# When VectorE makes the V index of a separately gathered expert row: in the row's own step, or in the next one

## The chip, the cores and the metric

One Trainium2 chip, one core. The metric is device time of one execution in microseconds (us). The kernel before takes 1458.97 us (median of three runs, 1458.47 to 1459.36).

## The reference, cut to what matters

The reference is a chain of two transformer blocks on 256 tokens of width 1024. The change touches only the last part, the mixture of single-vector experts at the end of the second block. There every token has 8 heads, each head picks 16 of 16384 experts, and each expert is one row of `expert_u` and one row of `expert_v` (1024 float32 numbers each, 4 KB):

```
best, pos = lax.top_k(cand, K)                      # K = 16
idx = jnp.take_along_axis(cand_idx, pos, axis=-1)
g = jax.nn.softmax(best, axis=-1)
u = expert_u[idx]
v = expert_v[idx]
act = jax.nn.gelu(jnp.einsum('td,thkd->thk', xt, u))
return jnp.einsum('thk,thkd->td', (g * act), v)
```

For one token and one expert this is a dot product with the U row, a gelu, a weight, and the weighted V row added to the sum. Where the gelu comes out as zero, the V row isn't needed.

## The kernel before, in words

Tokens lie on the 128 partitions, in two blocks of 128. The work of this last stage is cut into 256 "rows": row i = 16n + k is the expert of rank k of group n, where a group is one head of one token block (16 groups, `GROUPS`, of 16 ranks, `EXPK`). The program runs as five separate instruction streams that meet only in semaphores. Per row they do this:

- **GpSimd (POOL)** issues the gathers. There are 8 buffers (`SLOTS`), and row i uses buffer i mod 8. Rows in buffers 1, 4 and 7 (`JOINT`) are fetched in one gather of 8 KB per token, U and V together, from a table that was joined beforehand (`row`, L665). Rows in buffers 0, 2, 3, 5 and 6 are separate: one gather for U (L672), and a later one for V (`row_v`, L682), which skips the tokens whose weight is zero. The V gather of row r stands in POOL's stream six rows later (`V_LAG`), just behind the U gather of row r + 6. It waits until VectorE has made the V index of row r (`rows_picked`), and until TensorE has used the V rows that lay in the same buffer before (`row_used`). A U gather waits until VectorE has done the dot of the row eight earlier (`dot_ready`). The last eight rows are all fetched jointly.
- **VectorE (DVE)** waits for the row to land and multiplies and sums it with the token's vector (`row_dot`, L2596, 1.22 us). Between the dots it does one piece of the top-k selection of a coming group (`top_part`, L2477 to L2548), and for a separate row it makes the V index (`pick_row`): it waits for the weight of the row (`w_ready`), marks the tokens with weight zero (L2605) and adds that mark to the expert number, so that such a token lies beyond the table's end (L2610).
- **ScalarE (ACT)** does for each row a gelu of the dot (L1762), its product with the softmax probability (L1767, this releases `w_ready`), and it spreads the weight of a row over a 128 by 128 diagonal matrix (L1754): that of a joint row in the row's own step, that of a separate row seven steps later. Once per group, behind rank 2 (in group 0 behind rank 10), it does the exponentials of the next group's softmax (`exp_best`, L1747). Exponential and gelu are in different function tables, so a table is loaded before it and another one behind it.
- **TensorE (PE)** multiplies the diagonal with the V row and adds to the sum (`weigh_row` L1288, and L1331 in the rolled loop of rows 144 to 247): a joint row in its own place, a separate row r when row r + 8 has its turn. The order is fixed. In groups 0 to 7 it also makes the queries and scores of later groups in between.

VectorE's order in one step k of group n is written out by hand: the dot of row k; then the V index of row k - 1; then the other pieces (`decode`, `top_part`, at rank 6 or 14 also `probabilities`). So the V index of a row was made behind the dot of the next row.

Of the kernel before, what the change touches and what calls it, by code (L numbers as in the profile page):

```python
# [42 lines left out]
EXPK = 16  # L43
# [5 lines left out]
SLOTS = 8  # L49

JOINT = (1, 4, 7)
# [147 lines left out]
def two_blocks(nc, wstream, x_t, mem_t, cols, const, head_gains, c_rows, positions, w_krope, w_uq, w_ukv,  # L199
               w_rg, w_ig, sub_keys, w_ada, expert_u, expert_v, out):  # L200
    with ExitStack() as ctx:
# [294 lines left out]
        def separate(rows):  # L496

            return rows // SLOTS * (SLOTS - len(JOINT)) + sum(k not in JOINT for k in range(rows % SLOTS))

        def joint(i):  # L500
            return i % SLOTS in JOINT or i >= LAST_FROM
# [194 lines left out]
        def _(pe):  # L696
# [203 lines left out]
            def first_block(layer):  # L900
# [19 lines left out]
                for s, (kind, c, _) in enumerate(FUSED[:-KC]):  # L920
                    u = FUSED_AT[layer] + s
                    if kind == "v":
                        pair_half(bank["v", c | 1], u, c % 2, x)
                    else:
                        product = (lambda: chunk_sum(7, SQ, start_units, 3)) if (layer, s) == (0, 0) else None
                        proj(bank[kind, c], u, x, fresh, by="vec", fine_first=kind == "qm", between=product)
                        fresh = (None, None)
                        if layer and s == 0:
                            chunk_sum(7, steps=3)
                    taken[kind, c] = made["act" if kind == "v" else "vec"]  # L930
                    if kind == "qm":
                        pair_taken[layer, 6 + c] = (("vec", taken[kind, c]), ("act", taken["vm", 1]))
                    for p in range(6):
                        if (kind, c) == (("v", p + 1) if p % 2 == 0 else ("k", p)):
                            pair_taken[layer, p] = (("vec", taken["k", p]), ("act", taken["v", p | 1]))
                    if (kind, c) == ("qm", 1):
                        scale_by_token(layer + 1, RS)
                    if layer == 0 and (kind, c) == ("q", 1):
                        pe.wait_ge(fcum_ready, due(fcum_ready))
                    attend(layer, group_at[s], before, earlier)  # L940
                    if layer == 0 and (kind, c) == ("q", 1):
                        for b in range(NB):
                            mm = pe.transpose(PS[:, FQ_BANK, b * P:(b + 1) * P], FT[:, b * P:(b + 1) * P], ident)
                        mm.then_inc(tile_for["vec"], handed(FQ_BANK, "vec"))
                    before, earlier = group_at[s], before
# [421 lines left out]
        def _(act):  # L1367
# [82 lines left out]
            def first_block(layer):  # L1450
# [42 lines left out]
                for s, (kind, c, _) in enumerate(FUSED[:-KC]):  # L1493
                    if earliest is not None:
                        group_heads(layer, earliest)
                    if earlier is not None:
                        group_turned(layer, earlier)
                    if before is not None:
                        group_exps(layer, before)
                    split_hi(FUSED_AT[layer] + s + 2)  # L1500
                    if layer == 0 and s == 5:
                        forget_gate()
                    if (kind, c) == ("qm", 1):
                        take_scale(layer + 1)
                    elif kind == "v" and c % 2:
                        take_values(slice((c // 2) * T, (c // 2 + 1) * T), value_tile("v", c), layer + 1)
                    before, earlier, earliest = group_at[s], before, earlier
# [305 lines left out]
        def _(ve):  # L1813
# [768 lines left out]
            def probabilities(n):  # L2582
                par = n % 2
                ve.wait_ge(gexp_ready, n + 1)
                ve.reciprocal(gexp[:, par, 18:19], gexp[:, par, 16:17]).then_inc(topk_step, one(topk_step))
                if n >= 2:
                    ve.wait_ge(w_ready, EXPK * (n - 1))
                ve.wait_ge(topk_step, own(topk_step))
                ve.tensor_scalar(prob[:, par, :], gexp[:, par, 0:EXPK], gexp[:, par, 18:19], None,
                                 ALU.mult).then_inc(prob_ready, 1)  # L2590

            def row_dot(i):
                n, k = i // EXPK, i % EXPK
                row = place(i)[:, 0:D]
                ve.wait_ge(row_landed[i % SLOTS], 16 * (i // SLOTS + 1))
                ve.tensor_tensor_reduce(row, row, H2N[n // 8], 1.0, 0.0, ALU.mult, ALU.add,  # L2596
                                        dot[:, n % 2, k:k + 1]).then_inc(dot_ready, 1)

            def pick_row(i):

                n, k, s = i // EXPK, i % EXPK, i % SLOTS
                if joint(i):
                    return
                ve.wait_ge(w_ready, i + 1)
                ve.tensor_scalar(no_row[:, s:s + 1], wts[:, s:s + 1], 0.0, NO_ROW, ALU.is_equal,  # L2605
                                 ALU.mult).then_inc(tokens_marked, 1)
                if i >= SLOTS:
                    ve.wait_ge(v_landed[s], 16 * (i // SLOTS))
                ve.wait_ge(tokens_marked, separate(i + 1))
                ve.tensor_tensor(idx_v[:, s:s + 1], no_row[:, s:s + 1], idx[:, n % 3, k:k + 1],  # L2610
                                 ALU.add).then_inc(rows_picked, 1)

            def gated_sum(b, half=slice(0, 2)):
                cols = slice(half.start * 512, half.stop * 512)
                tmp = soft[:, 0:4 * T][:, cols]
                ve.tensor_tensor(tmp, PS[:, 2 * b + half.start:2 * b + half.stop, :].rearrange("p a e -> p (a e)"), G2[:, cols],
                                 ALU.mult).then_inc(vec_step, one(vec_step))
                ve.wait_ge(vec_step, own(vec_step))
                ve.tensor_tensor(XNAT[:, b, cols], XNAT[:, b, cols], tmp, ALU.add).then_inc(result_ready, 1)
# [6 lines left out]
            for n in range(GROUPS):  # L2626
                if n == 0:
                    probabilities(0)
                if n % 8 == 0:
                    ve.wait_ge(h2_ready, 2 * (n // 8 + 1))  # L2630
                for k in range(EXPK):
                    row_dot(n * EXPK + k)
                    if n or k:
                        pick_row(n * EXPK + k - 1)
                    if n == 0 and k == 0:
                        for q in range(6):
                            decode(0, q, slice(8, EXPK))
                    if n == 0 and 3 <= k < 9:
                        if k == 3:
                            ve.wait_ge(took["act"], QUERIES_FROM + 3)  # L2640
                        for q in range(3 * (k - 3), min(3 * (k - 2), EXPK)):
                            top_part(1, q)
                    if k >= TOPS_FROM and n + 2 < GROUPS:
                        if n < 6 and k == TOPS_FROM:
                            ve.wait_ge(took["act"], SCORES_FROM + 3 * (n + 3))
                        top_part(n + 2, k - TOPS_FROM)
                    elif 0 < n < GROUPS - 1 and k < TOPS_FROM:
                        top_part(n + 1, k + EXPK - TOPS_FROM)
                    if n == 1 and k < KC:
                        ve.tensor_scalar(DGATE[:, k * P:(k + 1) * P], ident, mod[:, 40 + k:41 + k], None,  # L2650
                                         ALU.mult).then_inc(g2diag, one(g2diag))
                    if k == (6 if n else 14) and n + 1 < GROUPS:
                        probabilities(n + 1)
                    if n == 9 and k == 8:
                        ve.wait_ge(took["act"], FINAL_TAKEN)
                        ve.wait_ge(row_used, weighed_by[last_weighed[0]])
                        gated_sum(0)
# [122 lines left out]
```

## Time and profile before

| | |
|---|---|
| median of three runs | 1458.97 us |
| profiled execution, its own time | 1459.09 us |
| its span | 1457.5 us |
| PE busy | 1373.4 us (94%) |
| DVE busy | 1150.3 us (79%) |
| ACT busy | 785.1 us (54%) |
| POOL busy | 499.1 us (34%) |
| DMA | 542.73 MB, mean 372 GB/s |

The profile is of one execution. The row stage runs from about 859 us (first gather) to 1449 us (last dot), 40% of the span. POOL is idle before the stage but for plain copies; within it, it issues 411 gathers. DMA is the mean busy share of the 16 DMA engines, and GB/s what they moved. A wait in the trace is written as [us idle <-what ended it] behind the instruction that it held up; for a wait on several semaphores the one named is the last to come by the profile.

### The profile page before, as it was taken

The numbers are of one execution on the slowest core, as the hardware profiler recorded it, in microseconds if no ns is written. First come the engines' busy times: TensorE is split into PE (matmuls) and PEld (weight loads), VectorE is DVE, ScalarE is ACT, GpSimd is POOL, SyncE is SP. The second block draws the span as 40 slices with busy tenths as digits, with TensorE's granted clock in tenths as the row PEclk, the third lists the DMA queues.
The fourth block names the chain that finished last, engine by engine and source line by source line (L and its number), as shares of the span: only waits on it lengthen the run. The fifth ranks groups of instructions, "written<-read, shape, count | busy, mean of one in ns | idle before, by whom it ended". The sixth has DMA issues, their size and how long they took to land.

```text
span 1457.5 us, 25909 instructions
## 1 busy us (share of the span) xinstructions
PE 1373.4 (94%) x8512; PEld 1067.3 (73%) x8512; DVE 1150.3 (79%) x2772; ACT 785.1 (54%) x1768; POOL 499.1 (34%) x600
## 2 busy tenths in 40 slices
PE   9999999999999999999999999999898998888878
PEld 9898999999989999998998985444454433333333
DVE  7777788878878888678799779887777778778764
ACT  6656544456556444456885535455555454455443
POOL 1111011110110111010111026776667676767672
PEclk9999999999999999999999999999999999999999
DMA  9999999999999999999999959999999999999997
GB/s 365 342 352 334 350 413 389 400 390 357 349 351 357 370 396 400 378 386 344 339 346 339 349 191 362 402 408 399 403 396 410 396 404 409 392 401 406 401 409 308
DMA packets 141598, 542.73 MB, mean 372 GB/s; under 512 B 22654, under 2 KB 22798, under 8 KB 128064
## 3 DMA queue, kind: packets, MB, share of 16 engines
q0 software_dynamic: 101904, 396.41, 72.3%
q1 hardware_dynamic: 38880, 141.92, 25.7%
q10 hardware_dynamic: 720, 3.24, 0.6%
q8 instruction: 47, 0.77, 0.2%
q14 instruction: 47, 0.39, 0.1%
HBM read 576.08 MB, written 135.27 MB: 488 GB/s over the span
## 4 chain that ended last, share of the span: by engine, by line
PE 60%; DMA 17%; DVE 11%; ACT 4%; issue 4%; POOL 4%; POOLq 0%; DVEq 0%; ACTq 0%
PE PS L757 10%; PE PS L748 10%; PE PS L740 10%; DMA late<-expert_uv,idx 8%; DMA attn<-expert_uv,idx 6%; PE PS L1288 5%; PE PS L788 3%; PE PS L1004 3%; PE PS L1000 3%; PE PS L1005 3%; PE PS L891 3%; DVE late L2596 2%; DVE attn L2596 2%; DMA attn<-expert_u,idx 2%; PE PS L1239 2%
## 5 line engine op out<-in xcount | busy, mean ns | idle before, releaser
L1398 ACT ACTIVATE early_splits<-ring 128x1024 fp32r<-128x1024 f32 x166 | 175.1, 1056 | 128.2 <-PE PS L748 99.2
L1856 DVE TENSOR_TENSOR early_splits<-ring,early_splits 128x1024 fp32r<-128x1024 f32 x166 | 202.5, 1221 | 32.9 <-ACT early_splits L1398 32.7
L1762 ACT ACTIVATE gel<-dot,token_rms 128x1 f32<-128x1 f32 x256 | 75.2, 294 | 255.4 <-DVE dot L2596 253.6
L2596 DVE CUSTOM_DVE_ANT_0 late<-late,PS 128x1024 f32<-128x1024 f32 x125 | 151.8, 1215 | 58.8 <-DMA late<-expert_uv,idx 58.5
L2596 DVE CUSTOM_DVE_ANT_0 attn<-attn,PS 128x1024 f32<-128x1024 f32 x125 | 151.9, 1215 | 35.6 <-DMA attn<-expert_uv,idx 29.3
L1288 PE MATMUL PS<-late,wrg 128*128 128x512 f32 x284 | 133.7, 598 | 19.2 <-ACT wrg L1754 19.0
L1288 PE MATMUL PS<-attn,wrg 128*128 128x512 f32 x288 | 133.8, 595 | 6.8 <-ACT wrg L1754 5.7
L1331 PE MATMUL PS<-late,wrg 128*128 128x512 f32 x208 | 103.3, 621 | 32.8 <-ACT wrg L1754 32.7
L672 POOL DMA_INDIRECT attn<-expert_u,idx x93 | 87.6, 942 | 98.9 <-DVE idx L2548 70.4
L682 POOL DMA_INDIRECT attn<-expert_v,idx_v x93 | 93.0, 1000 | 72.6 <-issue 26.3
L1288 PEld LDWEIGHTS PS<-late,wrg 128*128 128x128 f32 x284 | 51.2, 190 | 87.8 <-issue 87.6
L608 POOL DMA_DIRECT2D expert_uv<-expert_v x49 | 27.0, 552 | 238.4 <-DMA expert_uv<-expert_u 229.4
L1331 PEld LDWEIGHTS PS<-late,wrg 128*128 128x128 f32 x208 | 38.2, 193 | 92.2 <-ACT wrg L1754 53.9
L1331 PE MATMUL PS<-attn,wrg 128*128 128x512 f32 x208 | 97.0, 600 | 9.2 <-ACT wrg L1754 9.2
L1288 PEld LDWEIGHTS PS<-attn,wrg 128*128 128x128 f32 x288 | 52.4, 190 | 68.3 <-issue 68.3
L1398 ACT ACTIVATE late_split<-ring 128x1024 fp32r<-128x1024 f32 x65 | 68.6, 1056 | 61.9 <-PE PS L748 35.7
L1004 PE MATMUL PS<-product_split,early_splits 128*128 128x256 f32 x344 | 97.3, 283 | 0.0
L1000 PE MATMUL PS<-product_split,early_splits 128*128 128x256 f32 x344 | 96.8, 281 | 0.0
L1005 PE MATMUL PS<-product_split,early_splits 128*128 128x256 f32 x344 | 96.8, 281 | 0.0
L1754 ACT ACTIVATE wrg<-con,wts 128x128 f32<-128x128 f32 x248 | 88.7, 392 | 9.1 <-PE PS L1288 0.4
L608 POOL DMA_DIRECT2D expert_uv<-expert_u x49 | 27.0, 551 | 192.6 <-DMA expert_uv<-expert_v 191.8
L1856 DVE TENSOR_TENSOR late_split<-ring,late_split 128x1024 fp32r<-128x1024 f32 x65 | 79.3, 1219 | 13.8 <-ACT late_split L1398 13.8
(467 smaller groups left out, 3368.5 us busy)
## 6 DMA issues: line engine op xcount, KB each, us to landing
ring<-wstream SPq DMA_DIRECT2D x256, 512.0 KB, 9.0
expert_uv<-expert_u POOLq DMA_DIRECT2D x64, 1024.0 KB, 15.0
expert_uv<-expert_v POOLq DMA_DIRECT2D x64, 1024.0 KB, 15.0
ada<-w_ada POOLq DMA_DIRECT2D x32, 512.0 KB, 10.3
late<-w_ada POOLq DMA_DIRECT2D x16, 512.0 KB, 11.7
late<-wstream SPq DMA_DIRECT2D x4, 512.0 KB, 10.6
attn<-expert_u,idx POOLq DMA_INDIRECT x93, 8.6
attn<-expert_v,idx_v POOLq DMA_INDIRECT x93, 7.7
```

Of the source, the lines that this page charges most:

```text
L682: gp.indirect_dma_start(UV[s][:, D:2 * D], None, expert_v, bass.IndirectOffsetOnAxis(ap=idx_v[:, s:s + 1], axis=0), bounds_check=NKEYS * N ...
L740: mm = pe.matmul(out, hi_of(u)[:, k * P:(k + 1) * P], xl[:, k, :], start=False, stop=last and k == KC - 1)
L748: mm = pe.matmul(out, hi_of(u)[:, k * P:(k + 1) * P], xh[:, k, :], start=(k == 0), stop=False)
L757: mm = pe.matmul(out, lo_of(u)[:, k * P:(k + 1) * P], xh[:, k, :], start=False, stop=fine_first and k == KC - 1)
L1000: mm = pe.matmul(out_o, whi, FH[:, par, :], start=first and o % 2 == 0, stop=False, skip_group_check=True)
L1004: pe.matmul(out_o, wlo, FH[:, par, :], start=False, stop=False, skip_group_check=True)
L1005: mm = pe.matmul(out_o, whi, FL[:, par, :], start=False, stop=last, skip_group_check=True)
L1288: mm = pe.matmul(PS[:, 2 * b + g, :], diagonal(r), place(r)[:, D + g * 512:D + (g + 1) * 512], start=r == first_weighed[b], stop=r == last ...
L1331: mm = pe.matmul(PS[:, 2 * (first // (8 * EXPK)) + g, :], DIAG[:, m, :], UV[m][:, D + g * 512:D + (g + 1) * 512], start=False, stop=False, ...
L1398: act.activation(hi_of(u), raw(u), ACT.Copy).then_inc(hi_ready, 1)
L1856: ve.tensor_tensor(lo_of(u), raw(u), hi_of(u).bitcast(F32), ALU.subtract).then_inc(units_begun, 1)
L2596: ve.tensor_tensor_reduce(row, row, H2N[n // 8], 1.0, 0.0, ALU.mult, ALU.add, dot[:, n % 2, k:k + 1]).then_inc(dot_ready, 1)
```

## The change

Only the place of `pick_row` in VectorE's step changes. For a separate row whose successor is a joint row (buffers 0, 3 and 6, so ranks 0, 3, 6, 8, 11 and 14) the V index is now made at the end of the row's own step, ahead of the dot of the joint row. For buffers 2 and 5, whose successors are separate rows, it stays behind the next row's dot. The instructions, the semaphores and their counts are the same.

```diff
                 for k in range(EXPK):
                     row_dot(n * EXPK + k)
-                    if n or k:
+                    if (n or k) and k % SLOTS not in JOINT:
                         pick_row(n * EXPK + k - 1)
...
                     if k == (6 if n else 14) and n + 1 < GROUPS:
                         probabilities(n + 1)
+                    if (k + 1) % SLOTS in JOINT:
+                        pick_row(n * EXPK + k)
                     if n == 9 and k == 8:
```

## Rows read from the trace of the kernel before

**Rows 1.** Busy time by stretch: us, then PE, PEld, DVE, ACT, POOL, PEclk, DMA share, GB/s

```profile
884.00:916.00 32.00, 30.56 (x122) 17.45 (x120) 27.71 (x92) 19.95 (x54) 20.80 (x22) 1.00 0.94 344
916.00:1396.00 480.00, 420.43 (x1167) 193.56 (x1168) 384.80 (x1210) 243.17 (x720) 335.13 (x347) 0.99 1.02 403
1396.00:1446.00 50.00, 43.82 (x98) 17.76 (x97) 26.87 (x60) 21.25 (x68) 27.03 (x29) 1.00 1.02 414
```

**Rows 2.** The dots of L2596: what VectorE's idle time before them waited for (us, times)

```profile
  DMA late<-expert_uv,idx: 58.5, 45
  DMA attn<-expert_uv,idx: 29.3, 28
```

**Rows 3.** Timeline (start us, us, engine, line), row 168, rank 8, buffer 0

```profile
1248.85 1.21 DVE L2596 CUSTOM_DVE_ANT_0 attn<-attn,PS 128x1024 f32<-128x1024 f32 x1
...
1250.44 0.29 ACT L1767 ACTIVATE wts<-gel,prob 128x1 f32<-128x1 f32 x1
...
1252.35 1.22 DVE L2596 CUSTOM_DVE_ANT_0 attn<-attn,PS 128x1024 f32<-128x1024 f32 x1 [1.87 <-DMA attn<-expert_uv,idx]
...
1253.75 0.16 DVE L2610 TENSOR_TENSOR idx_v<-no_row,idx 128x1 uint32<-128x1 f32 x1
...
1254.70 1.00 POOL L682 DMA_INDIRECT attn<-expert_v,idx_v  x1 [0.65 <-issue]
```

**Rows 4.** POOL's V gathers of L682: idle time before them (us, times)

```profile
  DVE idx_v L2610: 24.9, 13
```

**Rows 5.** Timeline, row 195, rank 3, buffer 3, and the V gather of row 197

```profile
1308.97 1.21 DVE L2596 CUSTOM_DVE_ANT_0 late<-late,PS 128x1024 f32<-128x1024 f32 x1
...
1309.86 1.28 ACT L1747 ACT_TABLE_LOAD   x1
...
1311.67 1.28 ACT L1762 ACT_TABLE_LOAD   x1
...
1311.93 1.22 DVE L2596 CUSTOM_DVE_ANT_0 late<-late,PS 128x1024 f32<-128x1024 f32 x1 [1.31 <-DMA late<-expert_uv,idx]
...
1313.29 0.29 ACT L1767 ACTIVATE wts<-gel,prob 128x1 f32<-128x1 f32 x1
...
1313.62 0.15 DVE L2605 TENSOR_SCALAR no_row<-wts 128x1 f32<-128x1 f32 x1 [0.46 <-ACT wts L1767]
...
1314.64 1.98 PE L1331 MATMUL PS<-late,wrg 128*128 128x512 f32 x4 [1.19 <-ACT wrg L1754]
...
1319.84 1.00 POOL L682 DMA_INDIRECT attn<-expert_v,idx_v  x1 [0.31 <-issue]
```

**Rows 6.** All table loads of L1747: duration ns min/median/max, first and last start

```profile
L1747 ACT ACT_TABLE_LOAD  x15: 1283/1283/1283, 893.7 to 1381.4; - x15
```

**Rows 7.** Timeline, behind row 179, rank 3, in group 11

```profile
1277.27 1.22 DVE L2596 CUSTOM_DVE_ANT_0 late<-late,PS 128x1024 f32<-128x1024 f32 x1 [2.27 <-DMA late<-expert_uv,idx]
...
1277.67 0.29 ACT L1767 ACTIVATE wts<-gel,prob 128x1 f32<-128x1 f32 x1
```

**Rows 8.** Timeline of VectorE in group 0, around rows 0 to 2 and 12

```profile
869.02 1.21 DVE L2596 CUSTOM_DVE_ANT_0 attn<-attn,PS 128x1024 f32<-128x1024 f32 x1
...
870.59 0.15 DVE L2605 TENSOR_SCALAR no_row<-wts 128x1 f32<-128x1 f32 x1 [0.35 <-ACT wts L1767]
...
870.85 1.21 DVE L2596 CUSTOM_DVE_ANT_0 attn<-attn,PS 128x1024 f32<-128x1024 f32 x1
...
894.77 1.20 DVE L2596 CUSTOM_DVE_ANT_0 late<-late,PS 128x1024 f32<-128x1024 f32 x1
...
897.45 0.15 DVE L2605 TENSOR_SCALAR no_row<-wts 128x1 f32<-128x1 f32 x1 [1.47 <-ACT wts L1767]
```

**Rows 9.** The U gathers of L672, from issue to landing

```profile
DMA to landing us min/median/max: 4.1/8.4/10.2
```

**Rows 10.** Timeline of POOL, the V gather of row 53 (rank 5)

```profile
995.28 0.99 POOL L682 DMA_INDIRECT attn<-expert_v,idx_v  x1 [2.69 <-DVE idx_v L2610]
```

**Rows 11.** Busy time by stretch, the 4 us behind that gather's issue

```profile
996.00:1000.00 4.00, 4.00 (x15) 2.09 (x14) 2.54 (x11) 1.48 (x6) 3.09 (x4) 1.00 0.96 353
```

## The prediction

> **What bounds the kernel now.** I read the busy time by stretch first, because the change acts only in the row stage. From 916 to 1396 us the 16 DMA engines are busy all the time (share 1.02) and move 403 GB/s, while DVE has 385 of 480 us, ACT 243 and POOL 335 [rows 1]. PE has 420 of 480, so it is near, but it has gaps. This stretch is held by the gathers. The waits before the dots say the same: VectorE stands 87.8 us, in 73 places, for a joint row that hasn't landed [rows 2]. The stretch before is different. From 884 to 916 us DMA moves only 344 GB/s at a share of 0.94 while DVE is busy 27.7 of 32 us and PE 30.6 [rows 1]: there the engines hold back the gathers and not the other way round. Behind 1396 us, DMA moves 414 GB/s.
>
> So I ask two things. In the long stretch, does the change make DMA's supply of work better or worse? And in the first 50 us of the stage, does it make VectorE earlier or later?
>
> **What moves, in an ordinary step.** The change removes nothing and adds no instruction. Of the 155 V indices, the 93 of buffers 0, 3 and 6 (31 turns of 8 rows, 3 each) go from behind the joint row's dot to ahead of it. Row 168 is such a row [rows 3]. Its dot starts at 1248.85 and ends at 1250.07; its weight is there at 1250.73, 0.66 us later. DVE then stands 1.87 us for the joint row until 1252.35, and only behind that dot makes the index, which is done at 1253.91. POOL issues the V gather 0.79 us later, after a wait of 0.65. With the change the index is made in the 1.87 us in which DVE stands idle anyway: done at about 1251.1, 2.8 us earlier. The pair of instructions takes from 0.26 us (870.59 to 870.85 [rows 8]) to 0.34 us (end of the dot at 1253.57 to 1253.91 [rows 3]); I take 0.34. It costs nothing here, and DVE has 0.34 us less to do behind the joint dot. Where there is no such idle time, DVE pays 0.34 us ahead of the joint dot and gets it back behind it.
>
> What this can give is POOL's time: 24.9 us in 13 waits before V gathers are put down to the index [rows 4]. But the one row that I can check against it says otherwise. The gather at 995.28 with its 2.69 us [rows 10] is of row 53, buffer 5, whose index does not move. Such waits belong to TensorE freeing the buffer, or to an index that stays where it was. And POOL's wait is worth something only where DMA runs dry, which at a share of 1.02 is seldom. I put the gain from earlier gathers at 0.5 us.
>
> **The wait that is added: rank 3.** The index needs the row's weight, and now every joint dot behind buffers 0, 3 and 6 needs it too. Ordinarily that is 0.66 us. At rank 3 it isn't, as ACT does the next group's exponentials between ranks 2 and 3, with a table load on each side. The dot of row 195 ends at 1310.18; ACT loads tables at 1309.86 and at 1311.67, 1.28 us each, and the weight is there at 1313.58, 3.4 us behind the dot [rows 5]. Now the joint dot of row 196 starts at 1311.93, under this time, and the index finds its weight at 1313.62. With the change the index starts at 1313.62 again, and the dot of row 196 comes behind it, at 1313.62 + 0.34 = 1313.96: 2.03 us late. In row 179 the joint row itself landed late (1277.27), the weight at 1277.96, so the delay is 1277.96 + 0.04 + 0.34 - 1277.27 = 1.07 us [rows 7]. So 1.1 to 2.0 us, in each of the groups 1 to 14 (15 table loads [rows 6], less the one in group 0). What is queued behind it on DVE: the dots of rows 4 to 7, their top-k pieces and indices, later by the delay less 0.34. Who waits: ACT for the weight of row 4, then PE, which already stood idle 1.19 us for that diagonal [rows 5] and now stands longer, and then POOL, whose V gather of rank 5 needs the buffer that PE frees next. That gather was issued at 1319.84 with only the plain gap of 0.31 [rows 5], and against a later release I expect a wait of 1 to 1.7 us there.
>
> What does that cost in time? DMA has a store of work: a U gather takes 8.4 us to land in the median and 4.1 at least [rows 9], so some 4.3 us of each is queueing behind others. A POOL wait of 1 to 1.7 us eats into these 4.3 and isn't seen in the end time. But in some groups POOL already waits there: 2.69 us at 995.28, and the next 4 us move 353 GB/s in place of 403 [rows 10, 11], which is 4 x (1 - 353/403) = 0.5 us lost. A wait of some 4 us in place of 2.7 uses up the store; then each further us is lost whole. With three or four groups like that at 0.5 to 1 us each, and a little in the others, I take 2.5 us (from 0, all hidden, to 14 x (2.03 - 0.34) = 23.7, all passed on; I lie near the low end because of the store).
>
> The Trainium skill, page "DMA: Bandwidth & Descriptors", section "Anatomy of one DMA — SWDGE (gpsimd) path", gives a lone gather 2.0 us plus its bytes over 436 GB/s, 3.2 us for 512 KB; by that estimate the queueing would be 5.2 us and not 4.3, and the 2.5 us would fall to about 1.5. No row here shows a lone gather in the stage.
>
> The page "ScalarE: Activation LUTs", section "What ACT_TABLE_LOAD costs", puts a switch at 1283 ns for the load and about 1380 ns for a drain. The trace agrees on the load (1283 ns in all 15), but not on the drain: from the start of one load to that of the next, exponentials included, it is 1.81 us. With two drains the delay at rank 3 would be 2.8 us longer.
>
> **The wait that is added: group 0.** Here nothing hides it, since DMA waits for the engines. The dot of row 1 started at 869.02, but row 0's weight comes only at 870.55, since ACT was busy with other things; the index starts at 870.59, after 0.35 us of waiting [rows 8]. With the change the dot of row 1 comes behind it, and the dot of row 2 behind that, at 870.59 + 0.34 + 1.21 = 872.14 in place of 870.85: 1.3 us. The same again at rank 11, where group 0 has its table loads: the dot of row 12 was done at 894.77 under ACT's work, and DVE then waited 1.47 us more [rows 8]. Now that dot comes behind the wait: 1.2 us. That is 2.5 us of VectorE in a stretch where it is busy 87% of the time and sets the pace together with PE; between 0 (PE's queue covers it) and 2.8 (with a small wait at rank 8), I take 2.5.
>
> **The sum.** 1459.1 (the profiled execution's own time, 1457.5 of it span, and 0.1 above the median) + 2.5 (group 0) + 2.5 (rank 3 in 14 groups) - 0.5 (earlier gathers) = 1463.6. I say 1464 us, 0.3% slower.
>
> **Rivals.**
> 1. *The store of gathers hides it all.* Both the delays and the gains vanish behind DMA, but for 0 to 2 us of group 0: 1459 to 1461, say 1460. For it: share 1.02 throughout. Against: 344 GB/s in group 0. Chance 0.23.
> 2. *Faster.* The mechanism is POOL's run-ahead: V gathers of buffers 0, 3 and 6 are released up to 2.8 us earlier, the waits in front of them go, and DMA never thins out. The ceiling is 480 us at 414 GB/s in place of 403, 12.8 us; a third of it less group 0's loss gives 1459.1 - 4.2 + 1.2, about 1456. It decides if the dips come from late V gathers of these buffers more than from rank 5. Row 168's 0.65 us speaks for it, row 53 against. Chance 0.14.
> 3. *The delay at rank 3 passes on whole.* PE has 420 of 480 us of work, so it may not catch up 1.7 us in a group: 1459.1 + 2.5 + 23.7 = 1485. Against: PE's 12% of free time is 4 us per group of 34. Chance 0.06.
> 4. *The change doesn't do what it says*: the indices are made early but no V gather leaves earlier, since POOL has other things ahead of it; and DVE's delays fall into its waits. That is rival 1's time, and its chance is in there.
>
> My forecast has 0.57. The range, 1457.5 to 1474, holds the forecast with dips up to twice or three times my guess, rival 1, and a part of rival 2. A difference under 0.2%, 2.9 us, can't be told from none. Slower by more: most of the forecast and rival 3, 0.62. Within: rival 1 and the low edge of the forecast, 0.25. Faster: 0.13.
>
> **What would show it.** In the changed kernel: DVE's idle before L2605 (ACT's weight) grows from a few us to some 40 (14 times about 3 us less what parts lie before, plus group 0); the joint dots of rank 4 wait on no DMA in groups 1 to 14; PE stands about 1 us or more longer at rank 4; the V gather of rank 5 waits over 1 us in most groups; the first 60 us of the stage move less than now; and waits of V gathers of buffer 0 get fewer. I am wrong if group 0 is over as early as before, if the GB/s from 916 to 1396 us stay at 403 or rise, or if PE takes no longer wait at rank 4.

## The result, and the profile after

The changed kernel takes 1476.75 us (median of six runs, 1470.10 to 1481.61) against 1458.78 us: 1.0120 times as long, 95% interval 1.0105 to 1.0134. That is 17.5 us more; the two medians lie 18.0 us apart. The profiled execution took 1477.63 us, its span is 1476.0 us. The prediction had the right sign and the places of the two added waits, and gave the larger of them a sixth of its price.

By stretch, the columns as in [rows 1]:

```profile
884.00:916.00 32.00, 30.96 (x125) 18.04 (x124) 25.38 (x86) 19.26 (x50) 19.24 (x21) 0.99 0.91 324
916.00:1396.00 480.00, 414.89 (x1135) 193.08 (x1134) 375.73 (x1178) 233.18 (x695) 323.94 (x335) 0.97 0.99 388
1396.00:1446.00 50.00, 41.38 (x92) 16.66 (x90) 33.01 (x85) 23.24 (x71) 35.12 (x38) 0.99 1.03 412
```

The long stretch that DMA filled at 403 GB/s [rows 1] now moves 388, a loss of 480 x (1 - 388/403) = 17.9 us: nearly all of the difference lies there. The starts of the dots say the same. From row 16's dot to row 240's, groups 1 to 14, it is 504.9 us before and 521.8 after, 16.9 us more, of which groups 2 to 4 have 8.9; group 0 is 1.55 us longer. TensorE's granted clock has fallen from 0.99 to 0.97 in it. In the first stretch the rate went from 344 to 324 GB/s.

What VectorE waited for before its dots (L2596), to set beside [rows 2], and, in the second fence, before the marks of L2605 (us, times):

```profile
  DMA late<-expert_uv,idx: 28.8, 28
  DMA attn<-expert_u,idx: 14.9, 25
  DMA attn<-expert_uv,idx: 5.8, 11
```

```profile
  ACT wts L1767: 65.1, 54
```

The idle time before joint rows fell from 87.8 to 34.6 us. In its place VectorE waits 65.1 us for weights, up from 5.1 us in 9 waits. That alone costs little while DMA has gathers to work on (e14 below). What it does to the others is seen in the same place as [rows 5], rank 3 of group 12 (rows 195 to 197):

```profile
1325.41 1.28 ACT L1747 ACT_TABLE_LOAD   x1
...
1328.84 0.29 ACT L1767 ACTIVATE wts<-gel,prob 128x1 f32<-128x1 f32 x1
1329.16 0.15 DVE L2605 TENSOR_SCALAR no_row<-wts 128x1 f32<-128x1 f32 x1 [2.94 <-ACT wts L1767]
...
1329.50 1.22 DVE L2596 CUSTOM_DVE_ANT_0 late<-late,PS 128x1024 f32<-128x1024 f32 x1
...
1331.93 3.68 PE L1331 MATMUL PS<-late,wrg 128*128 128x512 f32 x4 [3.32 <-ACT wrg L1754]
...
1338.18 1.00 POOL L682 DMA_INDIRECT attn<-expert_v,idx_v  x1 [3.25 <-PE PS L1331]
```

The joint dot of row 196 comes behind the weight, as predicted. TensorE, which stood idle 1.19 us there, now stands 3.32 us, and the weighing behind it (x4 in the trace) takes 3.68 us where it took 1.98 [rows 5]. The V gather of rank 5 waits 3.25 us where it had the plain gap of 0.31. The stretches of that place show both the reason for the 3.68 and the cost of the 3.25:

```profile
1332.00:1334.00 2.00, 2.00 (x3) 0.97 (x4) 2.00 (x5) 1.05 (x4) 1.39 (x3) 0.50 1.00 408
...
1336.00:1348.00 12.00, 11.62 (x28) 4.81 (x26) 10.32 (x36) 4.94 (x17) 7.68 (x8) 1.00 0.96 356
```

After 3.32 us of idle time the granted clock is 0.50, that is 1.2 GHz in place of 2.4. The 12 us around and behind POOL's wait move 356 GB/s: 12 x (1 - 356/403) = 1.4 us lost in one group. In group 4, whose gather of rank 5 already waited 2.53 us in the kernel before, the wait is 5.89 us, and DMA is idle a third of the 10 us around it. The three rows are POOL's gather, TensorE's work between the weighing of row 68 and that of row 61, and the stretch:

```profile
1041.70 1.00 POOL L682 DMA_INDIRECT attn<-expert_v,idx_v  x1 [5.89 <-DVE idx_v L2610]
```

```profile
1036.03 3.09 PE L1239 MATMUL PS<-XN,ring 128*128 128x128 f32 x16
```

```profile
1040.00:1050.00 10.00, 10.00 (x36) 5.41 (x36) 6.42 (x26) 4.09 (x14) 6.47 (x7) 1.00 0.64 201
```

The POOL row names the index, but that index was made at 1036.39 us, 5.3 us earlier. What came last is the weighing of row 61, which had the buffer before and ended at 1040.84. In groups 1 to 4 TensorE makes a query at rank 4, between the two weighings: 1.95 us in group 4 of the kernel before, and 3.09 here, behind a wait of 3.15 us. So groups 2 to 4 came to the change with the longest waits, and lost most.

Read gather by gather in POOL's timeline, the waits before V gathers of rank 5 in groups 1 to 14 sum to 14.3 us before and 39.9 us after, 1.8 us more per group. This is close to what VectorE passes on: the step from the dot of rank 3 to that of rank 4 is 1.1 to 2.2 us longer, 1.7 in the mean. But it is spread unevenly. TensorE waited over 2 us for a diagonal twice in 916 to 1396 us before and in 13 places after, nine of them at rank 4. Behind nine of the 13 the granted clock fell; six of these nine are at rank 4, in groups 2, 4, 9, 11, 12 and 13. In these six groups the gather of rank 5 waits 3.1 us longer than before in the mean (2.6 to 3.5), in the other eight 0.85 us (0.1 to 1.3).

### The profile page after: what moved, and what is told of

It reads as the page before. It is cut to its first block, busy times and chain, and to the rows that moved or that the text cites. A ratio compares the mean times of both kernels' runs of the same rounds, so it can differ in the third digit from the quotient of the medians.

```text
span 1476.0 us, 25909 instructions
## 1 busy us (share of the span) xinstructions
PE 1382.1 (94%) x8512; PEld 1071.4 (73%) x8512; DVE 1153.0 (78%) x2772; ACT 784.4 (53%) x1768; POOL 499.6 (34%) x600
## 2 busy tenths in 40 slices
DMA packets 141598, 542.73 MB, mean 368 GB/s; under 512 B 22654, under 2 KB 22798, under 8 KB 128064
## 4 chain that ended last, share of the span: by engine, by line
PE 57%; DVE 15%; DMA 12%; ACT 8%; issue 4%; POOL 4%; SPq 0%; DVEq 0%; POOLq 0%; ACTq 0%
PE PS L757 10%; PE PS L748 10%; PE PS L740 10%; DMA attn<-expert_u,idx 8%; PE PS L1288 5%; DVE attn L2596 3%; DVE late L2596 3%; PE PS L788 3%; PE PS L1004 3%; PE PS L1000 3%; PE PS L1005 3%; PE PS L891 3%; PE PS L1239 2%; DMA late<-expert_uv,idx 1%; DMA ring<-wstream 1%
## 5 line engine op out<-in xcount | busy, mean ns | idle before, releaser
L2596 DVE CUSTOM_DVE_ANT_0 late<-late,PS 128x1024 f32<-128x1024 f32 x125 | 152.0, 1216 | 29.0 <-DMA late<-expert_uv,idx 28.8
L2596 DVE CUSTOM_DVE_ANT_0 attn<-attn,PS 128x1024 f32<-128x1024 f32 x125 | 151.9, 1216 | 21.6 <-DMA attn<-expert_u,idx 14.9
L1288 PE MATMUL PS<-late,wrg 128*128 128x512 f32 x284 | 137.8, 614 | 27.9 <-ACT wrg L1754 27.8
L1331 PE MATMUL PS<-late,wrg 128*128 128x512 f32 x208 | 106.1, 638 | 37.4 <-ACT wrg L1754 37.4
L682 POOL DMA_INDIRECT attn<-expert_v,idx_v x93 | 93.0, 1000 | 91.1 <-DVE idx_v L2610 26.0
L672 POOL DMA_INDIRECT attn<-expert_u,idx x93 | 88.2, 948 | 101.0 <-DVE idx L2548 71.9
```

Source lines behind the costliest of these rows:

```text
L682: gp.indirect_dma_start(UV[s][:, D:2 * D], None, expert_v, bass.IndirectOffsetOnAxis(ap=idx_v[:, s:s + 1], axis=0), bounds_check=NKEYS * N ...
L1288: mm = pe.matmul(PS[:, 2 * b + g, :], diagonal(r), place(r)[:, D + g * 512:D + (g + 1) * 512], start=r == first_weighed[b], stop=r == last ...
L1331: mm = pe.matmul(PS[:, 2 * (first // (8 * EXPK)) + g, :], DIAG[:, m, :], UV[m][:, D + g * 512:D + (g + 1) * 512], start=False, stop=False, ...
```

## The experiments

They were run in four sets, each beside the kernel before on the same chip; ratios are to it, with 95% intervals. Its own medians in the four sets were 1459.7 to 1461.3 us.

### Which ranks and groups: e1 to e4

The helper `in_own_step(i)` names the rows whose index is made in their own step; in the changed kernel it is `(i + 1) % SLOTS in JOINT`.

```diff
-                    if n or k:
+                    if (n or k) and not in_own_step(n * EXPK + k - 1):
                         pick_row(n * EXPK + k - 1)
...
+                    if in_own_step(n * EXPK + k):
+                        pick_row(n * EXPK + k)
# e1: (i + 1) % SLOTS in JOINT and not (n and k == 3)
# e2: (i + 1) % SLOTS in JOINT and n and k == 3
# e3: (i + 1) % SLOTS in JOINT and n == 0
# e4: (i + 1) % SLOTS in JOINT and n and k != 3
```

> The change without its rank 3: the V index of rank 3 in groups 1 to 15 stays behind the next row's dot, all other moved ones are moved. Theory (table loads): the loss is the wait at rank 3, where the weight comes 3.4 us behind the dot, so this comes out at 1458 to 1462 us, with the V gather of rank 5 waiting as in the kernel before. Rival (order): each joint dot that now stands behind a weight costs something, at all six ranks; then five of six ranks keep most of the loss, 1468 to 1475 us.

> The kernel before with only the V index of rank 3, in groups 1 to 15, made in its own step (15 of 155 indices). Theory (table loads): nearly the whole loss, 1472 to 1478 us, with step 3 of groups 1 to 14 about 5.0 us long. Rival (order, all six ranks): a sixth to a third of it, 1462 to 1465 us.

> The kernel before with the change in group 0 alone. The prediction gave group 0 2.5 us; the trace of the changed kernel has group 0 1.55 us longer (40.28 in place of 38.73 us). If this loss reaches the end: 1460 to 1462 us. Rival (it is caught up later, as the gathers are the bound behind it): 1458.5 to 1459.5 us.

> The change in groups 1 to 15 at all ranks but 3; group 0 as before. Theory (table loads): no added wait is left and the gathers of ranks 0, 6, 8, 11 and 14 are released earlier, so 1455 to 1459.5 us, not slower than before. Rival (order): 1466 us or more.

| | ratio | interval | median us |
|---|---|---|---|
| e1, all but rank 3 | 1.0011 | 1.0000 to 1.0021 | 1460.25 |
| e2, rank 3 alone | 1.0127 | 1.0103 to 1.0151 | 1476.33 |
| e3, group 0 alone | 1.0017 | 1.0007 to 1.0028 | 1461.81 |
| e4, groups 1 to 15 but rank 3 | 0.9997 | 0.9986 to 1.0009 | 1459.26 |

Moving 15 of the 93 indices gives the whole loss; moving the other 78 gives next to none. Group 0 costs 2.5 us (0.17%, 1.0 to 4.1 by the interval), which is the prediction's figure. The rival that each wait for a weight ahead of a joint dot is dear in itself falls. The earlier indices of ranks 0, 6, 8, 11 and 14 give nothing that can be measured. The long stretch of e2 and of e4, in this order:

```profile
916.00:1396.00 480.00, 413.18 (x1148) 192.07 (x1147) 374.27 (x1187) 237.83 (x704) 328.00 (x339) 0.99 1.00 393
```

```profile
916.00:1396.00 480.00, 420.53 (x1169) 192.99 (x1170) 390.51 (x1212) 243.21 (x722) 337.82 (x348) 1.00 1.02 405
```

### Is it the table loads: e5, e6 and e12

```diff
# e5 (on the changed kernel), e6 (on the kernel before), in exp_best(n)
+                if n:
+                    act.activation(gexp[:, par, 0:EXPK], best2[:, par, :], ACT.Copy,
+                                   scale=token_rms[:, 0, b:b + 1], accum_out=gexp[:, par, 16:17]).then_inc(gexp_ready, 1)
+                    return
# e12 (on the changed kernel)
-                    if n and k == 2 and n + 1 < GROUPS:
+                    if n and k == 9 and n + 1 < GROUPS:
                         exp_best(n + 1)
...
-                    if k == (6 if n else 14) and n + 1 < GROUPS:
+                    if k == 14 and n + 1 < GROUPS:
                         probabilities(n + 1)
```

e5 and e6 leave the exponentials of the softmax out from group 1 on, so their results are wrong; the bytes moved are the same, 542.73 MB.

> The changed kernel without table loads in the row stage: from group 1 on, the exponential of the softmax is left out (a copy takes its place, with the same sum), so the weight of rank 3 is no longer 3.4 us behind its dot. Theory (table loads): with them goes the loss; within 3 us of the same edit on the kernel before, and at 1455 to 1461 us. Rival (a weight waited for ahead of the joint dot of rank 4 is dear in itself): 1466 us or more.

> The kernel before with the same edit (exponential from group 1 on left out, no table loads in the stage), as the yardstick for the other. The weight of rank 3 was waited for behind a dot that had landed late, so both theories expect little: 1455 to 1459 us.

> The changed kernel with ScalarE's exponentials, and so the two table loads, behind rank 9 instead of rank 2 in groups 1 to 14, and VectorE's probabilities at rank 14 instead of 6. The weight of rank 3 is then 0.66 us behind its dot; that of rank 11 comes 2.4 us behind its own, so the joint dot of rank 12 is about 0.9 us late, in place of 2.0 at rank 4. Theory (table loads ahead of an index that is needed early): 1460 to 1466 us. Rival (order, wherever the loads stand): 1472 us or more.

Without table loads the changed order costs nothing that can be measured: e5 1.0002 (0.9982 to 1.0022), e6 1.0004 (0.9986 to 1.0021). Their difference is known to about 4 us, which leaves room for group 0. Both medians, 1461.43 and 1459.97 us, lie just above what I had given them. With the loads moved behind rank 9, e12 is at 1.0029 (1.0018 to 1.0041), 4.2 us, of which group 0 is 2.5. There the index of rank 11 finds its weight after a short wait, in group 12:

```profile
1326.71 0.15 DVE L2605 TENSOR_SCALAR no_row<-wts 128x1 f32<-128x1 f32 x1 [0.32 <-ACT wts L1767]
```

and the joint row behind it is still waited for, 1.05 us. So it is the loads, and only where an index that VectorE now needs early stands right behind them. Some 2 us for all 14 groups here (0 to 4 by the intervals), and 15 to 18.5 us at rank 3. The step from the dot of rank 11 to that of rank 12 is 1.1 us longer in the mean than in the kernel before, that of rank 3 in the changed kernel 1.7 us: the price is not proportional to the delay.

### Through which link: e7, e8, and TensorE's clock: e9 to e11, e13

e7 (on the changed kernel) and e8 (on the kernel before) weigh the separate rows of buffers 2 and 5 one place sooner, so that the V gather of rank 5 no longer depends on the late dot of rank 4:

```diff
# weighed_at(i), the order of TensorE; spread_at(i) (diagonals) is moved by one place likewise
-            return [r for r in (i - SLOTS, i) if r >= 0 and joint(r) == (r == i)]
+            early, late = i + 1 - SLOTS, i - SLOTS
+            out = [early] if early >= 0 and not joint(early) and early % SLOTS in (2, 5) else []
+            out += [late] if late >= 0 and not joint(late) and late % SLOTS not in (2, 5) else []
+            return out + ([i] if joint(i) else [])
```

> The changed kernel, but TensorE weighs the earlier separate rows of buffers 2 and 5 one place sooner, ahead of the joint row of buffer 1 or 4, and ScalarE makes their diagonals one place sooner. VectorE's wait at rank 3 stays as long. Theory (the chain: the late dot of rank 4 holds back TensorE's joint row, behind which the buffer of the V gather of rank 5 comes free, POOL stands, DMA runs dry): the link is cut, 1457 to 1463 us, and the wait before V gathers of rank 5 falls under 1.5 us. Rival (VectorE's lateness itself, or TensorE's clock): 1470 us or more.

> The kernel before with the same earlier place of the separate rows of buffers 2 and 5. Theory (chain): the waits of POOL before V gathers of buffers 2 and 5 shrink here too, 1452 to 1459 us. Rival: 1458 to 1461, no difference.

e8 is at 1.0000 (0.9979 to 1.0021), e7 at 1.0088 (1.0055 to 1.0121). Both miss the theory of the chain and come out at the rival's time. The wait before the gather of rank 5 did fall, to 0.3 to 1.65 us, as that theory said; but TensorE's idle time and its half clock stayed, in 11 places of the long stretch, and POOL's wait went to the gather of rank 8: 27.9 us in groups 1 to 14, against 4.8 in the changed kernel and 13.6 in e8. Those of rank 0 rose too, to 17.2 us, but stand at 17.0 in e8, which loses nothing. Nor does the half clock by itself cost anything that can be measured: e8 has it in six places of the long stretch and takes the time of the kernel before. Group 12 of e7, TensorE at rank 4 and then POOL at rank 8:

```profile
1322.75 3.68 PE L1337 MATMUL PS<-attn,wrg 128*128 128x512 f32 x4 [2.05 <-ACT wrg L1760]
```

```profile
1338.11 1.00 POOL L688 DMA_INDIRECT attn<-expert_v,idx_v  x1 [3.33 <-DVE idx_v L2616]
```

The first wait is for the diagonal of row 189, which e7 weighs first and which ScalarE makes behind the table loads; e8 waits 2.01 us at the same place. So e7 cut the link that it was meant to cut and added a wait of its own: it does not show that VectorE's lateness costs in itself.

To take the clock away, TensorE is kept busy while it waits, by two matmuls that add zero:

```diff
# e9 (changed kernel), e10 (kernel before), e11 (e7's order); rows from 144 on written out, without the loop
+            def keep_busy(b):
+                for g in range(2):
+                    pe.matmul(PS[:, 2 * b + g, :], blank[:], con[:, 0:512], start=False, stop=False, skip_group_check=True)
             def weigh(i):
+                if 16 < i < 240 and i % 16 == 4:
+                    keep_busy(i // 128)
                 for r in weighed_at(i):
+# e13 in place of that: here, if i % 16 == 4 and r == i
                     weigh_row(r)
```

> The changed kernel with two added matmuls of a zero matrix (about 0.94 us each) on TensorE at rank 4 of groups 1 to 14, ahead of its wait for the joint row's diagonal, where it stands idle 2 to 3.3 us; rows 144 to 239 are written out instead of looped. VectorE's wait stays. Theory (clock): part of the loss is that the granted clock of TensorE is 0.5 for about 3 us after such an idle time, so that the weighings behind it, which free the buffer of the V gather of rank 5, take twice as long; with the engine kept busy the 0.5 windows go and the time falls to 1464 to 1471 us. Rival (the 1.1 to 2 us of delay alone are the price): 1474 to 1479 us.

> The kernel before with the same two zero matmuls at rank 4 and the same writing out, as the yardstick. Its waits at rank 4 are mostly 1 to 1.9 us, so the matmuls fit, or delay the joint row by up to 0.9 us: 1457 to 1462 us on both theories.

> The changed kernel with both: the separate rows of buffers 2 and 5 weighed ahead of the joint row, and the zero matmuls at rank 4. Theory (chain and clock are the two parts of the price): 1459 to 1465 us, in spite of VectorE's wait at rank 3. Rival (VectorE's lateness itself costs): 1470 us or more.

> As e11, with the zero matmuls where they belong in that order: between the separate row that is weighed first and the joint row of rank 4, so that TensorE is busy in the wait that is left. e11 had them ahead of both and kept its half-clock windows. Theory (what was left in e7 and e11 is mostly the clock, which holds back the gathers of ranks 8 and 16): 1462 to 1468 us, next to no window with a granted clock of 0.5. Rival (lateness alone): 1470 us or more.

In e9 the granted clock is 1.00 in the whole stage, and the weighing of row 196 takes what it took before the change:

```profile
1322.81 1.88 PE L1277 MATMUL PS<-con,blank 128*128 128x512 f32 x4
1326.03 1.96 PE L1293 MATMUL PS<-late,wrg 128*128 128x512 f32 x4 [1.34 <-ACT wrg L1758]
```

The wait of the gather of rank 5 in that group is 1.29 us, down from 3.25. e9 is at 1.0093 (1.0065 to 1.0121), and e10, its yardstick with the same matmuls, at 1.0030 (1.0019 to 1.0041). So the change costs 0.6% between these two and 1.2% without the matmuls: by this the clock is worth about half, some 8 us of 17.5, with 5 us either way by the intervals. The yardstick isn't a clean one. In e9 the matmuls fit into TensorE's wait in nine of groups 1 to 13, in e10 in only two of 14, so e10 may carry more of their price than e9; and set against the kernel before, e9 is only 0.27% better than the changed kernel, 4 us. The uneven waits above give about half too: the six groups with half clock have 2.3 us more than the other eight, 13.7 of the 25.6 us that were added. So "about half" is an estimate, and 4 to 8 us what the times say.

The expected 1464 to 1471 us was missed narrowly (1471.76), and so was e10's 1457 to 1462 (1463.37); I had given the matmuls themselves no price. e11 (1.0083, 1.0066 to 1.0099) told little on the clock: its matmuls stood ahead of the wrong wait, and the long stretch has seven half-clock places, e7 11. e13 put them right and has three left there, and is at 1.0053 (1.0036 to 1.0070), in the middle between its two expectations.

### DMA's store: e14 to e16

```diff
-V_LAG = 6
+V_LAG = 7      # e14 on the changed kernel, e15 on the kernel before, e16 on e4
```

> The changed kernel with each V gather one row later in POOL's stream (behind the U gather of row r + 7, not r + 6). POOL then has one more gather out, some 1.3 us of DMA work, when it comes to the wait for the buffer of the V gather of rank 5. Theory (the loss is DMA's store running out while POOL stands at that gather): 1463 to 1470 us. Rival (VectorE or TensorE are the bound at rank 4, whatever is in store): 1475 us or more.

> The kernel before with V gathers one row later in POOL's stream, as the yardstick. Its stretch from 916 to 1396 us moves 403 GB/s, so there is little to win: 1454 to 1460 us; a V row that lands too late for TensorE would make it 1462 us or more.

> V gathers one row later in POOL's stream, and the change in groups 1 to 15 at all ranks but 3: the two kernels' good parts together. Theory: the earlier indices take no wait of their own and POOL's waits get less, so the fastest of all, 1453 to 1458 us. Rival (no room left under DMA): 1458 to 1461 us.

e14 is at 0.9996 (0.9979 to 1.0014), better than the 1463 to 1470 us that I expected: one more gather out when POOL comes to its wait, and the loss is gone. Against its own yardstick e15 it is 0.24% slower, 3.5 us with 3 either way, in which group 0's 2.5 has room. VectorE still waits for the weight of rank 3, and TensorE's clock still drops, in seven places of the long stretch. POOL still waits, but less: 22.7 us before the gathers of rank 5 in place of 39.9, since it issues one more gather, 1.2 us, before it comes to the wait. In group 4, POOL at rank 5, the clock, and the stretch behind:

```profile
1039.96 1.00 POOL L682 DMA_INDIRECT attn<-expert_v,idx_v  x1 [3.78 <-DVE idx_v L2610]
```

```profile
1034.00:1036.00 2.00, 2.00 (x8) 1.48 (x7) 1.67 (x9) 0.59 (x2) 1.70 (x2) 0.50 1.04 426
1042.00:1050.00 8.00, 8.00 (x32) 4.58 (x31) 6.05 (x21) 3.46 (x12) 5.94 (x7) 1.00 0.98 366
```

Over the 10 us from 1038 us, which lie about this gather as the stretch of 201 GB/s lies about that of the changed kernel, e14 moves 379 GB/s. Its long stretch is back at 402:

```profile
916.00:1396.00 480.00, 425.56 (x1175) 198.45 (x1174) 389.50 (x1212) 245.59 (x722) 335.96 (x348) 0.98 1.01 402
```

Its U gathers take 9.0 us to land in the median in place of 8.0 in the changed kernel. So VectorE's delay and TensorE's clock cost time through POOL's stand at a V gather, when DMA runs out of gathers meanwhile; without that they cost no more than the 3.5 us against e15.

e15 is the fastest kernel of all, 0.9972 (0.9958 to 0.9986), 1457.81 us: it beats the kernel before by 4 us. e16, with the early indices too, is at 0.9982 (0.9969 to 0.9994), 1458.62 us, in its rival's range and not faster than e15; the early indices give nothing here either.

## Why the prediction was wrong, step by step

- *DMA bounds the long stretch, the engines the first one*: right, and it explains the result, since nearly all of the loss is GB/s from 916 to 1396 us.
- *An ordinary step costs nothing and gives 0.5 us*: right within what can be measured (e4, 0.9997).
- *Group 0, 2.5 us*: right within its interval (e3, 2.5 us, 1.0 to 4.1). The hit on the figure is partly luck. In the trace each of the two delays is about 1.1 us, in place of the 1.3 and 1.2 predicted, and 0.7 us is caught up between them: at the end of group 0 VectorE is 1.55 us late.
- *The wait at rank 3, joint dot late by 1.1 to 2.0 us in 14 groups*: right in place, cause and length. VectorE waits 2.94 us for row 195's weight, and the step from row 195's dot to row 196's is 4.99 us, against 2.96 [rows 5]: 2.03 us late. Group 11, given 1.07 us, has 1.07 (a step of 4.99 us in place of 3.92).
- *What that costs, 2.5 us of a possible 23.7*: this step failed. The price is about 15 us (e2, 18.5 us, 15.0 to 22.0; the result less group 0, 15; the trace, 16.9 in groups 1 to 14). It had two parts.
  - "I expect a wait of 1 to 1.7 us there" (the V gather of rank 5): it was 3.25 us in group 12, 2.9 us longer than before. Over the 14 groups it was 2.9 us in the mean, of which 1.0 stood there before. So passing VectorE's delay on one to one was right in the mean (1.8 us added for a delay of 1.7), but not group by group. TensorE's idle time, with 1.19 us already standing, grew past 2 us in ten of the groups, and in six its clock went to half behind it: the weighing took 1.7 us more in group 12, and the wait 3.1 us more in the mean of the six. The kernel before had shown it: TensorE's only two waits over 2 us in the long stretch, 2.58 and 2.06 us, were each followed by a stretch of half clock; I had read PEclk only as a mean. Half clock stands for about half of the loss, as an estimate.
  - "4.3 us of each is queueing", so a wait of 1 to 1.7 us "isn't seen in the end time": the store was taken as full each time. Groups 2 to 4 came to it with 2.1 to 2.7 us already spent, and I gave them 0.5 to 1 us each; they lost 8.9 us, and group 4 had a stretch at 201 GB/s. With the store one gather larger the loss is gone (e14), so the mechanism, a wait that is free until DMA runs dry, was right and its size wrong.
- The Trainium skill's page "DMA: Bandwidth & Descriptors", section "Anatomy of one DMA — SWDGE (gpsimd) path", led to an estimate of a store of 5.2 us and a smaller loss. The runs speak against such a use of it: a median over all gathers says nothing of the gathers out at the moment of the wait, and waits of 3.25 us already cost 1.4.
- The Trainium skill's page "ScalarE: Activation LUTs", section "What ACT_TABLE_LOAD costs", has a drain of some 1380 ns at each switch. In the changed kernel too none is seen: in group 12 the first load starts at 1325.41 and the weight of rank 3 ends at 1329.13, 3.7 us, and two loads of 1.28 us, an exponential of 0.40 us with its sum of 0.19, the gelu and the product of 0.29 each fill all of it.
- *Rival 3, all passed on, 1485 us, chance 0.06*: 15 of its 23.7 us came, so the truth lay nearer to it than to the forecast. Its reason, TensorE can't catch up, was not the one: with the same delay TensorE had the room in e14, DMA had lost its work. Its 23.7 us took all groups at 2.03 us; the steps of the 14 groups grew by 23.9 in all.
- *Rival 2, faster*: it did not come, and its sum doesn't stand as written. Less group 0's loss of 2.5 us in place of 1.2 it gives 1457.4 and not 1456.
- *The signs*: fewer joint dots waiting on DMA, TensorE's longer stand, the longer wait of the gather of rank 5 and the slower first stretch all came; VectorE's waits for weights came to 65 us, more than the 40 I gave. One sign did not come: V gathers of buffer 0 had a wait over 0.4 us seven times before and seven times after.

Open: how large the clock's part is, between 4 us and somewhat over half; how the rest of the loss divides between the delay itself and the gathers' spread over the DMA engines; why some waits over 2 us are followed by half clock and others are not; and why e13 kept three half-clock places.

## What to carry to other kernels

Before a wait is moved ahead of work, look at the latest arrival of what it waits for, not the usual one: here 0.66 us behind the dot of an ordinary row, and 3.4 at the rank behind the table loads. Where a saturated queue seems to hide a delay, look at its lowest level, at the places where its issuer already stands: here groups 2 to 4 paid over half. And the depth of that queue (here one constant) can be worth more than the order of the work that feeds it: it took away a loss of 17.5 us, and gave the kernel before 4 us.

## What the runs showed that I had not expected

An idle time of 2.1 to 3.3 us of TensorE was followed by a granted clock of 0.50 for some 3 to 4 us in nine of 13 places of the long stretch, and a weighing took 3.68 us there in place of 1.88 to 1.98. It is not a matter of the wait's length alone: in e15 waits of 3.04 and 2.38 us were followed by no drop. Two matmuls of zeros in the wait removed it (clock 1.00 in e9) and saved 1.7 us of that weighing. In the kernel before, where there was little to save, they cost 0.3%, together with rows 144 to 239 written out (e10).
